# Two transformer blocks on one core: the first row's root taken by itself, the first group norm's mean as four matmuls of rounded parts, and eight convolution taps moved from steps 19 and 20 to step 26

## The reference, cut to what matters

```python
def _rmsnorm(x, g):
    xf = x.astype(jnp.float32)
    y = xf * lax.rsqrt(jnp.mean(xf * xf, axis=-1, keepdims=True) + NORM_EPS)
    return (y * g.astype(jnp.float32)).astype(x.dtype)
...
def _conformer_conv_branch(a, a_gate, z, conv_w, conv_b, gn_g, gn_b):
    h = a * jax.nn.sigmoid(a_gate)
    h = lax.conv_general_dilated(
        h, conv_w[:, None, :].astype(h.dtype), window_strides=(1,),
        padding=[(CONV_WIDTH - 1, 0)], dimension_numbers=('NWC', 'WIO', 'NWC'),
        feature_group_count=E_B) + conv_b
    b_, s_, _ = h.shape
    hn = _normalize(h.reshape(b_, s_, B_GROUPS, E_B // B_GROUPS)).reshape(b_, s_, E_B)
    hn = (hn * gn_g.astype(jnp.float32) + gn_b.astype(jnp.float32)).astype(a.dtype)
    return jax.nn.silu(hn) * jax.nn.silu(z)
```

## Time and profile before

| | |
|---|---|
| median of 3 runs | 742.91 us (742.89 to 742.97) |
| the profiled execution's own time | 743.22 us |
| its span in the trace | 741.4 us |
| TensorE busy | 733.1 us, 99% of the span |
| VectorE busy | 564.0 us, 76% |
| ScalarE busy | 416.4 us, 56% |
| GpSimd busy | 141.5 us, 19% |
| granted TensorE clock, mean | 0.999 |

### The profile page before, as it was taken

The page is one execution under the profiler, slowest core; times in us unless marked ns, Lnnn a source line. Parts: engine busy times, 40 slices in busy tenths (PEclk is TensorE's granted clock), DMA queues, the critical chain, the costliest instruction groups (busy, mean ns, idle before and its releaser), DMA issues.

```text
span 741.4 us, 10553 instructions
## 1 busy us (share of the span) xinstructions
PE 733.1 (99%) x4056; PEld 630.5 (85%) x4056; DVE 564.0 (76%) x924; ACT 416.4 (56%) x524; POOL 141.5 (19%) x92
## 2 busy tenths in 40 slices
PE   8999999999999999999999999999999999999996
PEld 8888899888888888998888887878889888888885
DVE  6879999889786876789998875656956665665665
ACT  6745644587773656756665656654346444444444
POOL 3399787770000000000032400000000000000000
PEclk9999999999999999999999999999999999999999
DMA  9867566554564695574455655355654546546521
GB/s 324 269 176 219 175 211 215 171 169 154 189 203 138 227 365 161 171 227 148 139 183 187 197 170 189 126 186 194 214 171 152 182 177 227 174 166 226 186 98 57
DMA packets 101118, 139.26 MB, mean 188 GB/s; under 512 B 4657, under 2 KB 75217, under 8 KB 101074
## 3 DMA queue, kind: packets, MB, share of 16 engines
q1 hardware_dynamic: 98242, 133.68, 54.8%
q10 hardware_dynamic: 2352, 3.40, 1.3%
q0 software_dynamic: 480, 1.57, 0.8%
HBM read 134.46 MB, written 4.19 MB: 187 GB/s over the span
## 4 chain that ended last, share of the span: by engine, by line
PE 92%; DVE 5%; ACT 1%; issue 1%; DMA 1%; SPq 0%; DVEq 0%; ACTq 0%
PE sums L1822 19%; PE sums L1790 10%; PE sums L1825 10%; PE sums L1792 10%; PE sums L1791 10%; PE misc L1822 5%; PE misc L2265 4%; PE misc L2267 4%; PE misc L2268 4%; PE misc L1825 3%; DVE sums L1103 1%; PE misc L1791 1%; PE misc L1790 1%; PE misc L1792 1%; PE misc L1726 1%; DVE s_wlo L1034 1%
## 5 line engine op out<-in xcount | busy, mean ns | idle before, releaser
L590 ACT ACTIVATE s_whi<-s_raw 128x2048 fp32r<-128x2048 f32 x93 | 174.9, 1881 | 59.9 <-PE sums L1792 37.5
L1034 DVE TENSOR_TENSOR s_wlo<-s_raw,s_whi 128x2048 fp32r<-128x2048 f32 x69 | 154.2, 2235 | 56.3 <-ACT s_whi L590 55.9
L1822 PE MATMUL sums<-s_a_parts,s_whi 128*128 128x512 f32 x472 | 118.5, 393 | 0.2 <-DVE s_abc L1143 0.2
L538 POOL TENSOR_TENSOR s_wlo<-s_raw,s_whi 128x1024 fp32r<-128x1024 f32 x46 | 110.4, 2427 | 22.0 <-ACT s_whi L590 22.0
L1822 PEld LDWEIGHTS sums<-s_a_parts,s_whi 128*128 128x128 f32 x472 | 85.9, 189 | 17.3 <-issue 1.2
L1103 DVE SCALAR_TENSOR_TENSOR sums<-s_reg_d,s_vectors,sums 128x256 f32<-128x256 f32 x232 | 93.2, 483 | 0.0
L957 ACT ACTIVATE s_whi<-s_raw 128x2048 fp32r<-128x2048 f32 x29 | 55.7, 1919 | 62.4 <-PE sums L1825 49.0
L1790 PE MATMUL sums<-s_whi,s_b_parts 128*128 128x512 f32 (+1 forms) x196 | 77.2, 394 | 0.0
L1791 PE MATMUL sums<-s_wlo,s_b_parts 128*128 128x512 f32 (+1 forms) x196 | 76.0, 388 | 0.0
L1792 PE MATMUL sums<-s_whi,s_b_parts 128*128 128x512 f32 (+1 forms) x196 | 76.0, 388 | 0.0
L1825 PEld LDWEIGHTS sums<-s_a_parts,s_wlo 128*128 128x128 f32 x472 | 64.4, 190 | 4.6
(11 more groups left out here) (365 smaller groups left out, 1335.8 us busy)
## 6 DMA issues: line engine op xcount, KB each, us to landing
s_raw<-in_w_in SPq DMA_DIRECT2D x61, 1024.0 KB, 5.4
s_raw<-in_w_up SPq DMA_DIRECT2D x16, 1024.0 KB, 5.4
s_raw<-in_w_down SPq DMA_DIRECT2D x16, 1024.0 KB, 5.8
s_raw<-in_w_pa SPq DMA_DIRECT2D x6, 1024.0 KB, 5.1
s_raw<-in_w_pb SPq DMA_DIRECT2D x6, 1024.0 KB, 5.0
s_raw<-in_w_out SPq DMA_DIRECT2D x4, 1024.0 KB, 5.0
s_raw<-in_w_ple_gate SPq DMA_DIRECT2D x4, 1024.0 KB, 5.5
s_raw<-in_w_o SPq DMA_DIRECT2D x4, 1024.0 KB, 5.0
```

Of the source, the lines that this page charges most:

```text
L538: gp.tensor_tensor(wlo[:, c % SLOTS, cols], raw[:, c % SLOTS, cols], whi[:, c % SLOTS, cols].bitcast(F32), ALU.subtract).then_inc(Sm["pool ...
L590: act.activation(ring_view(whi, c), ring_view(raw, c), ACT.Copy).then_inc(Sm["hi_ready"], 1)
L1034: ve.tensor_tensor(dst, src, part.bitcast(F32), ALU.subtract).then_inc(Sm["lo_ready"], 1)
L1822: pe.matmul(bank, wt(k)[0], parts[:, k, :, :], start=k == 0, stop=False, skip_group_check=True)
```

## The change

There are four edits, and the names of some semaphores go together (`pT_lo`, `wsT_lo` and `bv_lo` become one counter, `early_lo`).

**Root of the first row block.** ScalarE takes the root of block 0 as soon as its own sum of squares is there, ahead of the squares of block 1. Those are now one ScalarE instruction over 1024 columns; VectorE's share of them is gone, and with it the two small VectorE instructions that followed.

**Unit 0's low weights.** VectorE writes the second half of them in two pieces of 512 words with two products in between, and TensorE waits for each piece where it needs it.

**Mean of the first four tiles.** ScalarE rounds the four tiles of `conv` into `mean_parts` (the second half of `b_parts`) in step 18, VectorE writes the remainder in step 19, and `conv_mean(0)` is four fp32r matmuls of 512 columns in place of four plain ones of 256.

**Taps.** Step 19 issues 4 taps in place of 9, step 20 issues 6, step 26 issues 17.

```diff
@@ -84,7 +84,7 @@
 WO = [c for c, (kind, _) in enumerate(UNITS) if kind == "wo"]
 
 TAPS_A_STEP = 9
-TAPS_MORE = {FIRST["v"] + 1: 14, FIRST["za"]: 6}
+TAPS_MORE = {FIRST["v"] + 1: 14, FIRST["za"]: 6, FIRST["za"] + 3: -5, FIRST["za"] + 4: -3, FIRST["ga"] + 2: 8}
 GN_AT = 22
 GN_NEXT = 29
 POOL_WORDS = 1024
@@ -223,6 +223,7 @@
         reg_w = sb("reg_w", [P, UW])
         wsT = reg_w[:, 0:1024].rearrange("p (g i) -> p g i", g=KD)
         gn_sq = reg_w[:, 0:1024].rearrange("p (t s) -> p t s", t=NT)
+        mean_parts = b_parts[:, 4:8, :, :]
         wsT_hi, wsT_lo = b_hi[:, 4:8, :], b_lo[:, 4:8, :]
         bs_bc = reg_w[:, 1024:2048].rearrange("p (g i) -> p g i", g=KD)
         va = reg_w[:, 0:1024].rearrange("p (r n) -> p r n", r=NR)
@@ -247,6 +248,7 @@
         vec = vectors[:, 0:120]
         w_conv = vectors[:, 120:120 + TAPS * KD]
         vec2 = vectors[:, 120 + TAPS * KD:]
+        o128_r = o128[:, :].bitcast(F32R)
         fm = sb("fm", [P, KD])
         r_bc = sb("r_bc", [P, S])
         r8_bc = sb("r8_bc", [P, S])
@@ -593,15 +595,13 @@
             act.wait_ge(Sm["x_loaded0"], 16)
             act.activation(abc[:, 2 * UW:2 * UW + D], x_rows[:, 0, :], ACT.Square, accum_out=ssq[:, 0:1]
                            ).then_inc(Sm["ssq_ready"], 1)
-            act.wait_ge(Sm["x_loaded1"], 16)
-            act.activation(abc[:, 2 * UW + D:2 * UW + D + 512], x_rows[:, 1, 0:512], ACT.Square,
-                           accum_out=ssq[:, 1:2]).then_inc(Sm["ssq_ready"], 1)
             act.wait_ge(Sm["ssq_ready"], 1)
             act.activation(rstd[:, 0:1], ssq[:, 0:1], ACT.Sqrt, scale=1.0 / D, bias=EPS).then_inc(Sm["root_ready"], 1)
+            act.wait_ge(Sm["x_loaded1"], 16)
+            act.activation(abc[:, 2 * UW + D:3 * UW], x_rows[:, 1, :], ACT.Square, accum_out=ssq[:, 1:2]
+                           ).then_inc(Sm["ssq_ready"], 1)
             act.wait_ge(Sm["ssq_ready"], 2)
-            act.wait_ge(Sm["inv_ready"], 1)
-            act.activation(rstd[:, 1:2], ssq[:, 1:2], ACT.Sqrt, scale=1.0 / D, bias=rinv[:, 1:2]
-                           ).then_inc(Sm["root_ready"], 1)
+            act.activation(rstd[:, 1:2], ssq[:, 1:2], ACT.Sqrt, scale=1.0 / D, bias=EPS).then_inc(Sm["root_ready"], 1)
             act.wait_ge(Sm["first_loaded"], 16)
             def first_quarter(n):
                 cols = slice(UW // 4 * n, UW // 4 * n + UW // 4)
@@ -725,12 +725,18 @@
                     act.wait_ge(Sm["bv_zero"], 1)
                     act.activation(bias_hi, bias_v, ACT.Copy).then_inc(Sm["bv_hi"], 1)
                 if c == FIRST["u"] + 1:
-                    act.wait_ge(Sm["inv_ready"], 2)
+                    act.wait_ge(Sm["inv_ready"], 1)
                     act.activation(rstd[:, :], rinv[:, :], ACT.Sqrt).then_inc(Sm["root_ready"], 1)
                 if kind == "zb":
                     act.wait_ge(Sm["y_a"], j + 1)
+                    if j == 2:
+                        act.wait_ge(Sm["conv_mean"], 2)
                     act.activation(b_hi[:, 2 * j:2 * j + 2, :], mix[:, 2 * j:2 * j + 2, :], ACT.Copy
                                    ).then_inc(Sm["ya_hi"], 1)
+                if c == FIRST["za"] + 2:
+                    act.wait_ge(Sm["tap"], TAPS * NT)
+                    act.wait_ge(Sm["rowsum_mm"], 2)
+                    act.activation(mean_parts[:, :, 0, :], conv[:, 0:NT, :], ACT.Copy).then_inc(Sm["mean_hi"], 1)
                 if c == GN_AT + 1:
                     gn_square(0)
                 if c == GN_AT + 2:
@@ -1040,12 +1046,8 @@
                 return ap.rearrange("p (t s) -> p t s", t=2)
 
 
-            ve.wait_ge(Sm["x_loaded1"], 16)
-            link(ve.tensor_tensor_reduce(out=abc[:, 2 * UW + D + 512:3 * UW], in0=x_rows[:, 1, 512:D],
-                                         in1=x_rows[:, 1, 512:D], scale=1.0, scalar=0.0, op0=ALU.mult, op1=ALU.add,
-                                         accum_out=rinv[:, 0:1]))
-            ve.tensor_scalar(rinv[:, 1:2], rinv[:, 0:1], 1.0 / D, EPS, ALU.mult, ALU.add).then_inc(Sm["inv_ready"], 1)
             for r in range(NR):
+                ve.wait_ge(Sm[f"x_loaded{r}"], 16)
                 ve.wait_ge(Sm["root_ready"], r + 1)
                 ve.reciprocal(rstd[:, r:r + 1], rstd[:, r:r + 1]).then_inc(Sm["scale_ready"], 1)
                 ve.wait_ge(Sm["scale_ready"], r + 1)
@@ -1068,7 +1070,9 @@
                     first_lo(UW // 4, UW // 2, "first_lo")
                 if k == 4:
                     ve.wait_ge(Sm["second_hi"], 1)
-                    first_lo(UW // 2, UW, "lo_ready")
+                    first_lo(UW // 2, 3 * UW // 4, "first_lo")
+                if k == 6:
+                    first_lo(3 * UW // 4, UW, "lo_ready")
                 ve.wait_ge(Sm["in_hi"], k + 1)
                 ve.scalar_tensor_tensor(a_lo[:, k, :], M[k % 4][:, S * (k // 4):S * (k // 4) + S], col(vec, C_NORM + k),
                                         a_hi[:, k, :].bitcast(F32), ALU.mult, ALU.subtract
@@ -1205,6 +1209,9 @@
                              "ya_lo")
                 if c == GN_AT + 5:
                     gn_scale(0)
+                if c == FIRST["za"] + 3:
+                    ve.wait_ge(Sm["mean_hi"], 1)
+                    split_lo(mean_parts[:, :, 1, :], conv[:, 0:NT, :], mean_parts[:, :, 0, :], "mean_lo")
                 if c >= 3:
                     conv_taps(TAPS_A_STEP + TAPS_MORE.get(c, 0))
                 if c == GN_AT:
@@ -1918,9 +1925,9 @@
                     for n, (dst, cols) in enumerate(halves):
                         pe.matmul(dst, hs[:, k, cols], a_hi[:, k, :], start=k == 0 and n == 0, stop=False,
                                   skip_group_check=True)
-                    if k in (0, 2):
+                    if k in (0, 2, 4):
                         pe.wait_ge(Sm["first_lo"], k // 2 + 1)
-                    if k == KD // 2:
+                    if k == 6:
                         pe.wait_ge(Sm["lo_ready"], lo_count(0))
                     for dst, cols in halves:
                         pe.matmul(dst, ls[:, k, cols], a_hi[:, k, :], start=False, stop=False, skip_group_check=True)
@@ -1937,6 +1944,14 @@
                     pe.wait_ge(Sm["parts_added"], parts_count(FIRST["zb"]))
                 else:
                     pe.wait_ge(Sm["hn_ready"], 2)
+                if b == 0:
+                    pe.wait_ge(Sm["mean_lo"], 1)
+                    for h in range(2):
+                        for part in range(2):
+                            ins = pe.matmul(M[h][:, :], o128_r, mean_parts[:, 2 * h:2 * h + 2, part, :],
+                                            start=part == 0, stop=part == 1)
+                        ins.then_inc(Sm["conv_mean"], 1)
+                    return
                 for t in range(NT):
                     ins = pe.matmul(M[t // 2][:, S * (t % 2):S * (t % 2) + S], o128[:, :], conv[:, 4 * b + t, :],
                                     start=True, stop=True)
```

More of the change, by code:

```diff
@@ L300, in block_program @@
             ssq_ready inv_ready root_ready scale_ready second_hi numbers half_lo xr_ready first_loaded first_hi first_lo in_hi
-            in_lo xr_T xT_loaded pT_hi pT_lo wsT_sb wsT_hi wsT_lo rowsum_mm bs_ready
-            h_ready tap parts_copied parts_added conv_mean d_ready gsq_ready gvar_ready gstd_ready grcp_ready gbc_ready
+            in_lo xr_T xT_loaded pT_hi wsT_sb wsT_hi early_lo rowsum_mm bs_ready
+            h_ready tap parts_copied parts_added conv_mean d_ready mean_hi mean_lo gsq_ready gvar_ready gstd_ready grcp_ready gbc_ready
             hn_ready silu_ready yb_ready stats_v vn_ready mixed y_a ya_hi
@@ L311, in block_program @@
             mx_ready up_summed x3_ready mix_gated sel_ready branch_half m2_T out_half x1_rows x1_T x1_sq gate_half ple_scaled x2_rows x2_T x2_sq xg_rows xg_sq
-            diag_ready rbc_T wo_half x4_T x4_ready bv_zero bv_hi bv_lo mix_ready lam_exp lam_ready""".split()
+            diag_ready rbc_T wo_half x4_T x4_ready bv_zero bv_hi mix_ready lam_exp lam_ready""".split()
         sems = {n: sem(n) for n in names}
@@ L814, in _ @@
                 squares(x_res, 0, (1, r), "x1_sq")
-            act.wait_ge(Sm["inv_ready"], 3)
+            act.wait_ge(Sm["inv_ready"], 2)
             act.activation(r1_col[:, :], r1_sum[:, :], ACT.Sqrt).then_inc(Sm["root_ready"], 1)
@@ L842, in _ @@
                 squares(x_g, 2, (1, r), "xg_sq")
-            act.wait_ge(Sm["inv_ready"], 4)
+            act.wait_ge(Sm["inv_ready"], 3)
             act.activation(r23_col[:, :, :], r23_sum[:, :, :], ACT.Sqrt).then_inc(Sm["root_ready"], 1)
@@ L1160, in _ @@
                     ve.wait_ge(Sm["wsT_hi"], 1)
-                    split_lo(wsT_lo, reg_w[:, 0:1024].rearrange("p (t s) -> p t s", t=4), wsT_hi, "wsT_lo")
+                    split_lo(wsT_lo, reg_w[:, 0:1024].rearrange("p (t s) -> p t s", t=4), wsT_hi, "early_lo")
                     ve.wait_ge(Sm["pT_hi"], 1)
-                    split_lo(c_lo[:, 0:2, :], pT_raw, c_hi[:, 0:2, :], "pT_lo")
```

(11 more changed lines are left out.)

## The result

The changed kernel takes 744.59 us in the median of 13 runs (744.43 to 744.83), the kernel before 742.96 in as many: a ratio of 1.0022, 95% interval 1.0015 to 1.0029. That is 1.63 us slower, where +1.48 was worked out. Of all the runs behind the medians in this document two took far longer than the rest of their kernel, 4116 us for one of the nine with four taps moved and 906 us for one of the 31 of the kernel before beside it; without them these two medians are 744.58 instead of 744.62 and 742.97 instead of 742.98 us, and every ratio and interval here leaves them out. The profiled execution took 744.43 us. Its span grew by 1.2 us though TensorE is busy 1.4 us less than in the earlier trace rows.

What follows compares the result with a forecast made beforehand. TensorE, busy 99%, was taken as the bound, with VectorE's unbroken stretch before unit 29 level with it; -0.4 (roots) - 0.45 (low weights) - 0.81 (mean) + 3.14 (taps) = +1.48 us gave 744.4 us, range 743.3 to 745.2.

Steps and rivals of the forecast that it cites:

- The taps: Eight taps put into step 26, in VectorE's stretch without rest, were to delay unit 29 by their full 3.14 us.
- The first sum: TensorE's wait ahead of unit 28 for VectorE's addition of unit 26, forecast as 1.2 us.
- The second: TensorE's wait ahead of unit 29 for VectorE's addition of unit 27, forecast as about 1.9 us.
- Rival 2: The taps cost nothing, so the gains stand alone: -1.66 us, 741.25 us; chance 0.11.
- The mean: First mean on TensorE: four fast matmuls at 0.92 us replace 1.73 us on the chain, gain 0.81 us.
- The sentence on what the remainder could meet: VectorE's new subtraction in step 19 can meet a GpSimd subtraction and seem to stand still until that one is done.
- the bound of 3.6: Longest time for VectorE's subtraction in step 19 if it meets a GpSimd instruction: 1.22 + 2.39 = 3.6 us.
- The head: Up to the end of unit 0: earlier roots gain 0.4 us, split low weights 0.45 us, together 0.85 us.
- The sum: Whole kernel: -0.4 - 0.45 - 0.81 + 3.14 = +1.48 us, slower.
- Rival 1: The head gives nothing or little, only the mean counts: +2.3 us, 745.2 us; chance 0.12.
- Rival 3: VectorE's stretch shortens by itself, its cast giving back 0.58 us: +0.9 us, 743.8 us; chance 0.09.
- Rival 4: The mean has to wait behind the subtraction in step 19, losing from its 0.81 us: 745 us or more; chance 0.04.

## Why the prediction was right, point by point

**The taps (+3.14).** Right in size, place and waits. The chain has 3.13 us more, the move alone +3.13 us, taking it back -3.07. The two waits were forecast as 1.2 and 1.9 us and are 1.33 and 1.76. The first sum left out the 0.13 us between the end of the addition and TensorE's start (182.74 to 182.87 in the earlier trace rows). The second came out close because two terms that it left out nearly cancel: the wait of 0.20 us that was there before adds to it, and the slower start of unit 28 behind its own wait takes from it. The waits together grew by 2.89 us (3.09 against 0.20), and the rest of the 3.13 is that second start behind a wait. Rival 2, that the taps cost nothing, is out: four of them already cost 1.56 us on the chain.

**The mean (-0.81).** Right: 0.92 us in place of 1.73 on the chain, 0.86 us in the medians. The sentence on what the remainder could meet was right too, in the changed kernel's timeline (the remainder, and the rests in steps 21 and 25):

```profile
124.43 3.16 DVE L1043 TENSOR_TENSOR s_b_parts<-s_abc,s_b_parts 128x1024 fp32r<-128x1024 f32 x1
...
133.61 0.69 DVE L1147 TENSOR_TENSOR s_reg_e<-misc,s_reg_e 128x512 f32<-128x512 f32 x1 [1.50 <-ACT s_reg_e L668]
...
158.92 0.69 DVE L1147 TENSOR_TENSOR s_abc<-sums,s_abc 128x512 f32<-128x512 f32 x1 [0.98 <-ACT s_abc L668]
```

The subtraction of 1024 words took 3.16 us instead of 1.22, within the bound of 3.6. As the eight taps were gone, VectorE still rested 1.50 us in step 21. Without the move it was hidden as well, by less. GpSimd was at work beside it all the time, on the low weights of the units:

```profile
119.30 15.35 POOL L540 TENSOR_TENSOR s_wlo<-s_raw,s_whi 128x1024 fp32r<-128x1024 f32 x6 [1.92 <-ACT s_whi L592]
```

Six of these instructions at the 2.39 us of the earlier trace rows would be 14.3 us; they took 1.0 us more. Looked at singly, the one that was running when VectorE's subtraction began at 124.43 ended at 126.51, and VectorE's ended 1.08 us later, at 127.59; the next one on GpSimd began at 126.47, took 3.41 us and ended 2.29 us after VectorE's. So the trace agrees with the prediction's reading that one stands still until the other is done, and shows it on both engines in turn. The price was smaller than the bound because GpSimd's instruction had only 2.08 us left. No run was made with GpSimd idle there, so the cause rests on these times.

**The head (-0.85).** The mechanism was right, and the profiled pair showed more: 1.07 us. The scaling of block 1 came 0.63 us earlier instead of 0.4, because its squares could start at 5.80 where I had its rows arrive at 6.07 as before. They followed the root of block 0 without a wait for the rows, so here it was ScalarE's own work and not the arrival that set their start. The turning of block 0 began at 6.79 and not near 7.1, as it had only the scaled rows to wait for; that gives nothing, since the turning of block 1 began at 8.03. The arrival is no fixed time. In the timelines of the two kernels with moved taps and the old head, eight and then four taps moved, ScalarE begins the squares of block 1 at:

```profile
5.78 0.63 ACT L597 ACTIVATE s_abc<-s_abc 128x512 f32<-128x512 f32 x1 [0.17 <-DMA s_abc<-in_x]
```

```profile
6.21 0.63 ACT L597 ACTIVATE s_abc<-s_abc 128x512 f32<-128x512 f32 x1 [0.68 <-DMA s_abc<-in_x]
```

In the kernel with eight taps moved unit 1 began at 16.02. Against that the changed kernel's head is 0.80 us shorter. In the medians the parts gave 0.30 and 0.47 us, 0.77 together: the two pieces were sized 0.4 and 0.45.

**The sum.** +3.13 - 0.86 - 0.30 - 0.47 = +1.50 from the parts measured singly, +1.63 for all at once. The 0.13 us between are less than the intervals of a single comparison here, and I leave them open. The profiled execution of before lies 0.26 us above its median, that of the changed kernel 0.16 below its own: for that reason the two traces show +1.2 us and the medians +1.63.

**Rivals 1, 3 and 4.** The head gave its part. The cast in the stretch took 0.87 us again, so nothing came back there. The mean never waited.

## What to carry to other kernels

When an engine off the bottleneck works without rest between two points at which the bottleneck waits for it, a small wait, here 0.2 us, in the waits view can stand for a second critical path, and work moved into that stretch then costs its full length, as it did here, even if it is taken from elsewhere on the same engine. Look for the last rest ahead of such a stretch and the last result that is waited for at its end: the same eight instructions cost 3.1 us inside and 0.3 us right behind it, and the fastest kernel was the one that took two of the stretch's own instructions out of it and spread work over rests ahead of it. When an edit needs room for new work on an engine, first ask whether the rest behind it already gives that room: here it did, and the move that made room was the only part of the change that cost time.

## What the runs showed of the hardware that I had not expected

The arrival of the second half of x, with the same code and the same queue, moved between 5.78 and 6.21 us after the start in the profiled executions of the four kernels with the head of before (eight taps moved 5.78, the mean alone 5.90, before 6.07, four taps moved 6.21), and the end of unit 0 with it: unit 1 began 10.21 to 10.24 us after the arrival in all four. A head of a few microseconds that hangs on a DMA's arrival should be compared over several executions. And a matmul group behind a wait of 0.2 us took 0.25 us longer on the chain than its like (2.09 against 1.84 us), most of it the overlap of 0.16 us with the group before that a wait breaks; removing such a wait gave 0.48 us in the medians and 0.42 in the traces. Last, where VectorE's and GpSimd's subtractions met in step 19, GpSimd's was longer in its turn: after VectorE's had taken 3.16 us instead of 1.22, the GpSimd instruction beside it took 3.41 instead of 2.40.
